# Ten modulation runs of the odd layer: from TensorE matmuls to ScalarE scaling and GpSimd adds

## The chip, the core and the metric

The kernel runs on one core of one Trainium2 chip. The metric is the device time of one execution in microseconds (us). Its engines are PE (TensorE: matrix products), DVE (VectorE), ACT (ScalarE), POOL (GpSimd) and SP (SyncE, which issues the loads). PEld is TensorE's load of weights, which runs beside its products.

## The reference, cut to what matters

Two blocks run one after the other on a stream x of 256 tokens by 1024. The first is a mixer with a mixture of experts; the change doesn't touch it. The second has two layers (0 even, 1 odd), each steered by a modulation that is computed from one vector c:

```python
cond = silu(c)                                       # 1 x 1024
for l in range(2):
    mod = cond @ ada_w[l] + ada_b[l]                 # 1024 -> 6144
    sh1, sc1, g1, sh2, sc2, g2 = split(mod, 6)
    h = rms_norm(x, norm_mix[l]) * (1 + sc1) + sh1
    y = even_mixer(h) if l % 2 == 0 else odd_mixer(h)    # attention
    x = x + g1 * (y @ w_out[l])
    h = rms_norm(x, norm_ffn[l]) * (1 + sc2) + sh2
    x = x + g2 * ((silu(h @ wg) * (h @ wu)) @ wd)    # feed-forward, 2816 wide
```

`ada_w` is 2 x 1024 x 6144 in fp32, 48 MB. The kernel reads it in 24 loads of 2 MB; load v gives half of one of the six vectors: layer v // 12, half v % 12. Loads 22 and 23 are the two halves of the odd layer's g2.

## The kernel before

**Loads.** All weights of the second block pass through five slots of 2 MB (`ring`). SP issues the loads in the order of `plan.loads`; load k takes the slot of load k - 5 and waits until that one is `freed`: for a product's weights until their last chunk is used, for a modulation weight until its run is done. SP issues in order, so a load that waits holds up all behind it.

**Chunks.** A product's weights are used in chunks of 1024 columns, numbered from 0 over the whole program. ACT copies chunk i to one of six buffers (`W_c_r`, `X_c_r`: the high part), DVE subtracts the copy from the weights (`ring_r`: the low part), PE multiplies three times (high, low, and the high weights with the low part of h). `begin(i)` on each of the three engines is chunk i's step, and behind it stands whatever the plan puts at the point ("f", i). On PE begin(i) comes five chunks ahead of the use. The even feed-forward has the gate and up chunks 62 to 105, four for each of 11 loads, and the down chunks 106 to 127; the odd layer follows with its key/value weights (kvo) 128 to 131, its two query halves 132 to 139, sixteen attention units, the output product 140 to 147 and its feed-forward from 148.

**Modulation.** `Plan.ada` (l. 143) puts a *run* at a point: PE multiplies the eight 128x512 slices of load v by silu(c), repeated over 32 columns (`csr`), into bank 7; ACT copies the bank to `acc`. `Plan.close` puts the *close* at a later point: PE sums `acc` over the partitions with four one-column products by `ones`, or, for loads 22 and 23, in row form with two products of 512 columns (`acc,ones` and `gates,ones`); then DVE adds the bias into `modc`, or ACT copies the row to `gates`. Bank 7 is shared, so each run waits until the close before it has been read. The even layer's g2 is in `modc`.

**Places.** Run 14 stands inside the normalisation at the head of the even feed-forward (`modulated`, between the sums and the broadcast), run 15 and the close of 14 at chunk 112, the close of 15 at 115, run 16 inside the normalisation of the odd layer, runs 17 to 23 at units 0, 2, ..., 12 of the odd attention, the closes at the units between.

**Stage boundaries.** When a product has ended, DVE forms 1 + scale times the gain (`prepare`, two small operations on `st`), adds the gated result to x in eight steps (`add_xT`, `x<-ps,modc,x`), ACT squares (`sc<-x`), PE sums over the partitions (`ones,sc`), DVE forms the inverse root (`st`, then `rb`, printed as `sc<-st`), PE broadcasts it (`ident,sc`), DVE and ACT normalise in eight steps (`R_c<-x,st,ps`, `hT_r<-R_c,modc`), and the next product starts.

**Names in the rows.** L1826 is PE's one matmul helper and L32 the helper of DVE, ACT and POOL, so tiles tell the operations apart. L651 and L678 are the load issues of gate/up and of the other weights.

## Time and profile before

| | |
|---|---|
| median of 3 runs | 1469.51 us (1468.12 to 1473.89) |
| the profiled execution | 1468.73 us, span 1467.0 us |
| mean granted clock of PE | 0.88 of full speed |
| PE busy | 1191.2 us (81%) |
| DVE busy | 615.8 us (42%) |
| ACT busy | 475.6 us (32%) |
| POOL busy | 7.6 us (1%), 54 instructions |
| chain that ended last | PE 57%, DMA 22%, DVE 12%, ACT 5% |

The span lies within the profiled execution's own time. Shares are averages over stages with different limits: the DMA share of the chain comes from the experts of the first block. The even feed-forward runs from about 925 to 1130, the odd attention from about 1172 to 1240. Granted clock 1.00 is TensorE's upper level (2.4 GHz), 0.50 the lower (1.2 GHz).

### The profile page before, as it was taken

The numbers are of one execution on the slowest core, as the hardware profiler recorded it, in microseconds if no ns is written. First come the engines' busy times: TensorE is split into PE (matmuls) and PEld (weight loads), VectorE is DVE, ScalarE is ACT, GpSimd is POOL, SyncE is SP. The second block draws the span as 40 slices with busy tenths as digits, with TensorE's granted clock in tenths as the row PEclk, the third lists the DMA queues.
The fourth block names the chain that finished last, engine by engine and source line by source line (L and its number), as shares of the span: only waits on it lengthen the run. The fifth ranks groups of instructions, "written<-read, shape, count | busy, mean of one in ns | idle before, by whom it ended". The sixth has DMA issues, their size and how long they took to land.

```text
span 1467.0 us, 19464 instructions
## 1 busy us (share of the span) xinstructions
PE 1191.2 (81%) x7703; PEld 874.9 (60%) x7703; DVE 615.8 (42%) x1240; ACT 475.6 (32%) x767; POOL 7.6 (1%) x54
## 2 busy tenths in 40 slices
PE   5888888575676756846897888999999978999998
PEld 4665565242332323413675438899898735999986
DVE  3473652010010000101663676655535656565553
ACT  4561621000000000002532335555433447455541
POOL 1000000000000000000000000000000000000000
PEclk9897888798888878978897678899999988999999
DMA  8542149999999999999446431865546472655520
GB/s 294 173 150 80 59 168 424 430 429 430 431 429 428 431 430 428 431 425 401 164 152 244 172 116 58 264 204 203 191 151 223 174 274 70 222 181 187 205 98 29
DMA packets 121729, 368.67 MB, mean 251 GB/s; under 512 B 9842, under 2 KB 56093, under 8 KB 110878
## 3 DMA queue, kind: packets, MB, share of 16 engines
q1 hardware_dynamic: 120556, 367.26, 65.1%
q8 instruction: 64, 1.05, 0.3%
q10 hardware_dynamic: 1074, 0.08, 0.1%
q14 instruction: 35, 0.29, 0.1%
HBM read 366.28 MB, written 1.05 MB: 250 GB/s over the span
## 4 chain that ended last, share of the span: by engine, by line
PE 57%; DMA 22%; DVE 12%; ACT 5%; issue 3%; SPq 1%; DVEq 0%; ACTq 0%
PE ps L1826 54%; DMA more<-in_w_gate_dram 8%; DMA more<-in_w_down_dram 7%; DMA more<-in_w_up_dram 6%; PE ps L1830 3%; DVE st L32 3%; DVE ring_r L32 2%; DVE R_c L32 2%; SPq L669 1%; DVE X_c L32 1%; DVE R_a L32 1%; DVE X_a L32 1%; ACT W_c_r L32 1%; ACT X_c L32 1%; DVE sc L32 1%
## 5 line engine op out<-in xcount | busy, mean ns | idle before, releaser
L1826 PE MATMUL ps<-hT_r,ring_r 128*128 128x256 f32 x864 | 243.7, 282 | 0.0
L1826 PE MATMUL ps<-ring,xg 128*32 128x512 f32 x640 | 140.1, 734 | 126.1 <-DMA more<-in_w_gate_dram 79.3
L1826 PEld LDWEIGHTS ps<-ring,xg 128*32 128x32 f32 x640 | 36.9, 132 | 222.3 <-issue 222.3
L1826 PEld LDWEIGHTS ps<-hT_r,ring_r 128*128 128x128 f32 x864 | 166.0, 192 | 0.0
L32 DVE TENSOR_TENSOR ring_r<-ring,W_c_r 128x1024 fp32r<-128x1024 f32 x94 | 115.2, 1225 | 96.3 <-ACT W_c_r L32 92.4
L1826 PE MATMUL ps<-R_c_r,W_c_r 128*128 128x256 f32 x608 | 152.7, 283 | 0.0
L32 DVE TENSOR_TENSOR ring_r<-ring,X_c_r 128x1024 fp32r<-128x1024 f32 x88 | 107.8, 1225 | 95.2 <-ACT X_c_r L32 92.3
L1826 PE MATMUL ps<-R_c_r,X_c_r 128*128 128x256 f32 x576 | 147.7, 284 | 0.0
L1826 PE MATMUL ps<-more,xg 128*32 128x512 f32 x384 | 134.6, 726 | 0.0
L32 ACT ACTIVATE W_c_r<-ring 128x1024 fp32r<-128x1024 f32 x94 | 99.7, 1060 | 87.3 <-PE ps L1826 83.0
L32 ACT ACTIVATE X_c_r<-ring 128x1024 fp32r<-128x1024 f32 x88 | 93.3, 1061 | 89.6 <-PE ps L1826 84.4
L32 DVE TENSOR_TENSOR x<-x,ps 128x512 f32<-128x512 f32 x36 | 24.8, 688 | 231.3 <-PE ps L1826 231.0
L1826 PE MATMUL ps<-hT_r,X_c_r 128*128 128x256 f32 x416 | 118.3, 284 | 2.9 <-DVE R_c_r L32 2.5
L1826 PE MATMUL ps<-hT_r,W_c_r 128*128 128x256 f32 x416 | 118.6, 285 | 1.9 <-DVE R_c_r L32 1.8
L1826 PEld LDWEIGHTS ps<-R_c_r,W_c_r 128*128 128x128 f32 x608 | 108.8, 190 | 0.0
L1826 PEld LDWEIGHTS ps<-R_c_r,X_c_r 128*128 128x128 f32 x576 | 104.0, 191 | 1.5 <-issue 1.5
L1826 PE MATMUL ps<-ring_r,hT_r 128*128 128x512 f32 (+1 forms) x240 | 94.8, 395 | 0.0
L1826 PEld LDWEIGHTS ps<-hT_r,X_c_r 128*128 128x128 f32 x416 | 78.8, 189 | 4.4 <-issue 3.0
L1826 PEld LDWEIGHTS ps<-hT_r,W_c_r 128*128 128x128 f32 x416 | 79.7, 191 | 2.7 <-DVE R_c_r L32 2.2
L1826 PE MATMUL ps<-ring,csr 128*32 128x512 f32 x384 | 63.6, 794 | 13.1 <-DVE modc L32 12.6
L1826 PE MATMUL ps<-ring,hid 128*32 128x512 f32 x320 | 60.2, 654 | 12.7 <-DMA more<-in_w_down_dram 11.6
L1826 PE MATMUL ps<-sel,hn 128*128 128x128 f32 x256 | 63.1, 410 | 2.1 <-DVE sel L32 2.1
(280 smaller groups left out, 1912.4 us busy)
## 6 DMA issues: line engine op xcount, KB each, us to landing
ring<-in_ada_w_dram SPq DMA_DIRECT2D x24, 2048.0 KB, 8.1
ring<-in_w_gate_dram SPq DMA_DIRECT2D x20, 2048.0 KB, 18.9
ring<-in_w_up_dram SPq DMA_DIRECT2D x20, 2048.0 KB, 20.0
ring<-in_w_down_dram SPq DMA_DIRECT2D x20, 2048.0 KB, 19.4
more<-in_w_gate_dram SPq DMA_DIRECT2D x12, 2048.0 KB, 27.9
more<-in_w_up_dram SPq DMA_DIRECT2D x12, 2048.0 KB, 28.4
more<-in_w_down_dram SPq DMA_DIRECT2D x12, 2048.0 KB, 27.9
ring<-in_ffn_gate_dram SPq DMA_DIRECT2D x22, 1024.0 KB, 5.9
```

The lines of the kernel that those rows point to most:

```text
L32: op(*args, **kw).then_inc(sem, 1)
L669: sp.dma_start(dst, src).then_inc(s_w[slot[k]], 16)
L1826: return pe.matmul(out, lhsT, rhs, start=start, stop=stop, skip_group_check=True)
L1830: return pe.transpose(out, in_, ident[0:n, 0:n])
```

## The change

Runs 14 to 23 become *pool runs* (`pool_run`). For one that is planned when the chunk list has length c: at the points ("f", c + 2) to ("f", c + 5) ACT multiplies two of the eight slices each, in place in the ring, by 32 silu(c) of their rows (`cs32`, one more small tile, `ring<-ring,cs` in the rows); POOL waits for the last of them and for the close of the run before, and adds the eight slices into `acc` with seven 128x512 additions, each waiting for the one before; at ("f", c + 11) PE closes as before, for load 23 at the first attention unit. The slot of such a load is freed by POOL's last addition. The c are 62, 70, ..., 126 in steps of 8, and 132; the closes stand at 73, 81, ..., 137.

The order of the loads changes with it: modulation load 14 stands ahead of the first gate/up load, 15 to 19 behind every second gate/up load, 20 to 22 behind the down loads 0, 2 and 4, 23 behind kvo. The output weights of the odd layer move from unit 8 to ahead of attention. Seven runs and their closes leave the attention.

```diff
@@ -145,6 +145,16 @@
         v = self.pending = len(self.ada_order)
         self.ada_order.append((v // 12, v % 12, self.load("ada", v // 12, v % 12)))
         self.rows.setdefault(point, []).append((v, "run"))
+    def pool_run(self):
+        v, c = len(self.ada_order), len(self.chunks)
+        self.ada_order.append((v // 12, v % 12, self.load("ada", v // 12, v % 12)))
+        self.pooled.append(v)
+        for z in range(4):
+            self.rows.setdefault(("f", c + 2 + z), []).append((v, z))
+        self.rows.setdefault(("u", 4, 0) if v == 23 else ("f", c + 11), []).append((v, "close"))
     def product(self, name, n, part=None):
         k = self.load("w", name)
@@ -170,23 +180,21 @@
             if u == wo_at:
                 self.out_loads(j)
-    def ffn(self, l, turn_run, run):
+    def ffn(self, l, gate_up_runs=(), down_runs=()):
         self.first["gu", l] = len(self.chunks)
         for u in range(11):
             k = self.load("gu", l, u)
             for q in (0, 2, 1, 3) if u == 0 else range(4):
                 self.feed(k, q)
-            if u == 0 and turn_run:
-                self.ada(("n", l, 3))
+            if u in gate_up_runs:
+                self.pool_run()
         self.first["dn", l] = len(self.chunks)
         for u in range(6):
             k = self.load("w", ("dn", l, u))
             for q in range(min(4, 22 - 4 * u)):
-                if run is not None and 4 * u + q == run:
-                    self.ada(("f", len(self.chunks)))
-                if run is not None and 4 * u + q == run + 3:
-                    self.close(("f", len(self.chunks)))
                 self.feed(k, q)
+            if u in down_runs:
+                self.pool_run()
@@ -218,18 +226,18 @@
     p.units(3, 8, (0, 2, 4, 6), 2, 1)
     p.close(("o", 1))
     p.out_proj(1)
-    p.ffn(0, True, 6)
+    p.pool_run()
+    p.ffn(0, (1, 3, 5, 7, 9), (0, 2, 4))
     k = p.load("w", "kvo")
     p.first["kvo"] = len(p.chunks)
     for q in range(4):
         p.feed(k, q)
-    p.ada(("n", 1, 0))
+    p.pool_run()
     p.product("q0", 4)
     p.product("q1", 4)
-    p.units(4, 16, (0, 2, 4, 6, 8, 10, 12), 8, 2)
-    p.close(("o", 2))
+    p.out_loads(2)
     p.out_proj(2)
-    p.ffn(1, False, None)
+    p.ffn(1)
     p.end = len(p.chunks)
     return p
@@ -397,7 +406,7 @@
         for i, (k, q) in enumerate(plan.chunks):
             freed[k] = (s_use, i + 1)
         for v, (_, _, k) in enumerate(plan.ada_order):
-            freed[k] = (s_ar, v + 1)
+            freed[k] = (s_acp if v in plan.pooled else s_ar, v + 1)
         for m, k in enumerate(plan.experts):
             freed[k] = (s_mm, m + 1)
@@ -788,6 +797,15 @@
             side.end()
+            for v in plan.pooled:
+                w = ring[:, slot[plan.ada_order[v][2]], :].rearrange("p (c n) -> p c n", c=8)
+                pool.wait_ge(s_ar, v + 1)
+                pool.wait_ge(s_ac, v)
+                G(pool.tensor_tensor, acc[:, :], w[:, 0, :], w[:, 1, :], ALU.add)
+                for c in range(2, 8):
+                    G(pool.tensor_tensor, acc[:, :], acc[:, :], w[:, c, :], ALU.add, up=s_acp if c == 7 else None)
         @block.scalar
         def scalar(act):
@@ -804,10 +822,19 @@
             def ada(point):
                 for v, what in plan.rows.get(point, ()):
                     l, i, k = plan.ada_order[v]
-                    if what == "run":
+                    if what in range(4):
+                        w = ring[:, slot[k], :].rearrange("p (c n) -> p c n", c=8)
+                        if what == 0:
+                            act.wait_ge(*landed[k])
+                            if v == plan.pooled[0]:
+                                act.wait_ge(s_cs, 1)
+                                copy(cs32[:, :], cs[:, :], scale=32.0)
+                        for c in (2 * what, 2 * what + 1):
+                            copy(w[:, c, :], w[:, c, :], scale=cs32[:, c:c + 1], up=s_ar if c == 7 else None)
+                    elif what == "run":
                         act.wait_ge(s_ar, v + 1)
                         copy(acc[:, :], ps[7][:, :], up=s_acp)
-                    elif row_gate(l, i):
+                    elif what == "close" and row_gate(l, i):
                         act.wait_ge(s_ac, v + 1)
                         copy(gates[:, 512 * (i % 2):512 * (i % 2) + 512], ps[7][:, :], up=s_gate)
@@ -1832,6 +1859,8 @@
             def ada(point):
                 for v, what in plan.rows.get(point, ()):
                     l, i, k = plan.ada_order[v]
+                    if what in range(4):
+                        continue
                     take(7)
                     if what == "run":
                         w = ring[:, slot[k], :].rearrange("p (c n) -> p c n", c=8)
```

Three places show what the planner makes of it. The first is ACT at the head of the even feed-forward, before; `hT_r<-ps,st` ends the normalisation of the even attention's output, `sc<-x` are the squares at the boundary:

```order
L32 ACTIVATE X_c_r<-ring 128x1024 x2
L32 ACTIVATE W_c_r<-ring 128x1024
L32 ACTIVATE X_c_r<-ring 128x1024
L32 ACTIVATE sc<-x 128x256 x8
L32 ACTIVATE hT_r<-R_c,modc 128x256 x8
L32 ACTIVATE acc<-ps 128x512
L32 ACTIVATE W_c_r<-ring 128x1024 x2
```

and after:

```order
L32 ACTIVATE X_c_r<-ring 128x1024 x2
L32 ACTIVATE W_c_r<-ring 128x1024
L32 ACTIVATE cs<-cs 128x8
L32 ACTIVATE ring<-ring,cs 128x512 x2
L32 ACTIVATE X_c_r<-ring 128x1024
L32 ACTIVATE ring<-ring,cs 128x512 x2
L32 ACTIVATE sc<-x 128x256 x8
L32 ACTIVATE hT_r<-R_c,modc 128x256 x8
L32 ACTIVATE W_c_r<-ring 128x1024
L32 ACTIVATE ring<-ring,cs 128x512 x2
```

Four scales of load 14 now stand among the chunk copies ahead of the squares, the other four between the next copies; the copy of bank 7 to `acc` is gone.

The second place is POOL's stream at its end, with the semaphores that each instruction waits for; `R_c` is a mask in the even attention. Before:

```order
L32 MEMSET qcol 64x1 [waits s_pool]
L32 MEMSET qcol 64x1 [waits s_slopes] x35
L32 MEMSET R_a 128x512 [waits s_slopes,s_k_decayed]
L32 AFFINE_SELECT R_c<-R_c 128x128 [waits s_slopes,s_index_sum]
L32 AFFINE_SELECT R_c<-R_c 128x256 [waits s_index_causal,s_index_sum]
```

and after, where `s_ada_run` is ACT's last scale of a run and `s_ada_closed` PE's close of the run before:

```order
L32 MEMSET R_a 128x512 [waits s_slopes,s_k_decayed]
L32 AFFINE_SELECT R_c<-R_c 128x128 [waits s_slopes,s_index_sum]
L32 AFFINE_SELECT R_c<-R_c 128x256 [waits s_index_causal,s_index_sum]
L32 TENSOR_TENSOR acc<-ring 128x512 [waits s_index_causal,s_ada_closed,s_ada_run]
L32 TENSOR_TENSOR acc<-acc,ring 128x512 [waits s_pool] x6
L32 TENSOR_TENSOR acc<-ring 128x512 [waits s_ada_copied,s_ada_closed,s_ada_run]
```

Ten groups of seven additions have come to the end of POOL's stream.

The third place is DVE at the end of the even feed-forward, where the last subtractions are those of the kvo chunks. Before:

```order
L32 TENSOR_TENSOR ring_r<-ring,W_c_r 128x1024 x2
L32 TENSOR_TENSOR ring_r<-ring,X_c_r 128x1024 x2
L32 TENSOR_TENSOR ring_r<-ring,W_c_r 128x1024
L32 TENSOR_TENSOR ring_r<-ring,X_c_r 128x1024
L32 TENSOR_SCALAR st<-modc 128x8
L32 TENSOR_TENSOR st<-st,cols 128x8
L32 SCALAR_TENSOR_TENSOR x<-ps,modc,x 128x256 x8
```

and after:

```order
L32 TENSOR_TENSOR ring_r<-ring,W_c_r 128x1024 x2
L32 TENSOR_TENSOR ring_r<-ring,X_c_r 128x1024 x2
L32 TENSOR_TENSOR modc<-ps,cols 128x4
L32 TENSOR_TENSOR ring_r<-ring,W_c_r 128x1024
L32 TENSOR_TENSOR ring_r<-ring,X_c_r 128x1024
L32 TENSOR_SCALAR st<-modc 128x8
L32 TENSOR_TENSOR st<-st,cols 128x8
L32 SCALAR_TENSOR_TENSOR x<-ps,modc,x 128x256 x8
```

The update of `modc` behind the close of run 21 now stands ahead of the last two subtractions and of the gated sum.

## Rows read from the trace of the kernel before

**Rows 1.** Windows: even feed-forward in two parts, odd attention, its end.

```profile
core 0: us, PE busy (x) PEld busy (x) DVE busy (x) ACT busy (x) POOL busy (x), PEclk, DMA share, GB/s
925.00:1055.00 130.00, 128.17 (x1064) 126.75 (x1060) 78.20 (x91) 67.72 (x85) 0.00 (x0) 0.98 0.64 212
1062.00:1132.00 70.00, 69.48 (x577) 65.89 (x577) 30.22 (x41) 24.09 (x28) 0.00 (x0) 0.98 0.54 189
1193.00:1224.00 31.00, 31.00 (x249) 16.06 (x246) 20.29 (x80) 21.91 (x62) 0.00 (x0) 1.00 0.77 272
1234.00:1237.00 3.00, 2.29 (x18) 1.26 (x16) 1.27 (x2) 2.25 (x5) 0.00 (x0) 0.52 0.02 5
```

**Rows 2.** Timeline of SP (start, duration): gate/up load 0, modulation load 14.

```profile
860.89 0.37 SPq L651 DMA_DIRECT2D ring<-in_ffn_gate_dram  x1
906.55 0.37 SPq L678 DMA_DIRECT2D ring<-in_ada_w_dram  x1
```

**Rows 3.** Load issues near 988 and 1010: KB, us to landing.

```profile
ring<-in_ffn_up_dram SPq DMA_DIRECT2D x1, 1024.0 KB, 8.0
...
ring<-in_ffn_down_dram SPq DMA_DIRECT2D x1, 2048.0 KB, 9.1
```

**Rows 4.** Timelines, head of the even feed-forward (start, us, idle before); a copy.

```profile
915.09 4.39 DVE L32 SCALAR_TENSOR_TENSOR x<-ps,modc,x 128x256 f32<-128x256 f32 x8
...
923.90 0.42 DVE L32 SCALAR_TENSOR_TENSOR sc<-st 128x256 f32<-128x256 f32 x1
...
922.22 3.64 PE L1826 MATMUL ps<-ring,csr 128*32 128x512 f32 x16
925.79 1.22 PE L1826 MATMUL ps<-ident,sc 128*128 128x128 f32 x4
928.78 0.36 PE L1826 MATMUL ps<-hT_r,X_c_r 128*128 128x256 f32 x1 [1.77 <-DVE R_c_r L32]
...
1047.57 0.63 ACT L32 ACTIVATE R_c_r<-sc 128x512 fp32r<-128x512 f32 x1 [1.43 <-DVE sc L32]
```

**Rows 5.** Timeline of PE at chunk 112: run 15.

```profile
1062.29 2.55 PE L1826 MATMUL ps<-ring,csr 128*32 128x512 f32 x16 [3.37 <-DVE modc L32]
```

**Rows 6.** Timeline of PE in the odd attention: a close, half a row close.

```profile
1204.99 1.05 PE L1826 MATMUL ps<-ones,acc 128*128 128x1 f32 x8
...
1216.60 1.12 PE L1826 MATMUL ps<-acc,ones 128*128 128x512 f32 x2
```

**Rows 7.** Timelines of DVE and PE at the boundary to the odd layer.

```profile
1123.63 4.39 DVE L32 SCALAR_TENSOR_TENSOR x<-ps,modc,x 128x256 f32<-128x256 f32 x8
...
1126.27 3.63 PE L1826 MATMUL ps<-ones,sc 128*128 128x1 f32 x32
...
1134.46 0.47 PE L1826 MATMUL ps<-X_c_r,hT_r 128*128 128x512 f32 x1 [1.77 <-DVE R_c_r L32]
```

**Rows 8.** Odd attention: DVE at units 3 and 15, a run, ACT's last pair.

```profile
1195.42 0.17 DVE L32 COPY X_c<-st 128x2 f32<-128x2 f32 x1
1230.03 0.17 DVE L32 COPY X_c<-st 128x2 f32<-128x2 f32 x1
...
1201.77 1.92 PE L1826 MATMUL ps<-ring,csr 128*32 128x512 f32 x16
...
1227.40 0.51 ACT L32 ACTIVATE X_c<-X_c,s 128x257 f32<-128x257 f32 x1
1231.65 0.51 ACT L32 ACTIVATE X_c<-X_c,s 128x257 f32<-128x257 f32 x1
```

**Rows 9.** Groups by line and shape: POOL's selects, DVE's subtraction, ACT's copy.

```profile
L32 POOL TENSOR_SCALAR_AFFINE_SELECT negd<-negd 128x256 f32<-128x256 f32 x1 | 0.4, 401 | 0.5 <-DVE negd L32 0.5
L32 POOL TENSOR_SCALAR_AFFINE_SELECT ident<-ident 128x128 f32<-128x128 f32 x1 | 0.3, 293 | 0.2 <-POOL ident L32 0.2
...
L32 DVE TENSOR_TENSOR ring_r<-ring,W_c_r 128x1024 fp32r<-128x1024 f32 x94 | 115.2, 1225 | 96.3 <-ACT W_c_r L32 92.4
...
L32 ACT ACTIVATE W_c_r<-ring 128x1024 fp32r<-128x1024 f32 x94 | 99.7, 1060 | 87.3 <-PE ps L1826 83.0
```

More of the change, by code:

```diff
@@ L125, in __init__ @@
     def __init__(self):
-        self.loads, self.ada_order, self.rows = [], [], {}
+        self.loads, self.ada_order, self.rows, self.pooled = [], [], {}, []
         self.chunks, self.first = [], {}
@@ L282, in build @@
         cs = sb("cs", [128, 8])
+        cs32 = sb("cs32", [128, 8])
         acc = sb("acc", [128, 512])
```

## The prediction

> **What bounds the kernel now.** I read the windows first, stage by stage, then the timelines at the stage boundaries, then the loads. In the even feed-forward PE is busy 128.2 of 130 us at a granted clock of 0.98, and 69.5 of 70 us in its second part [rows 1]: PE sets the pace, and whatever is added to its stream there is paid in full. A chunk of 1024 weight columns, 24 products, is used every 2.83 us (69.5 us less a close, for 577 products, gives 2.85, some cold ones among them); VectorE is busy 78 of the 130 us, ScalarE 68, GpSimd not at all. In the odd attention PE is again full, 31.0 of 31 us at clock 1.00 [rows 1], while the modulation runs are in it; behind the last run it falls to 0.52 [rows 1]. Between the stages stands a chain: the last chunks split on ScalarE and VectorE, VectorE adds the gated result to x, ScalarE squares, PE sums, VectorE normalises, PE starts [rows 4, 7]. So the change is worth what it does to PE in the two full stretches, to these chains, and to the loads, since the slot of a modulation weight now comes free only when GpSimd has done its adds.
>
> **The price of an add.** The whole case hangs on it. Call p the time of one of the 70 adds (128x512, each waiting for the one before). No row shows GpSimd adding two operands. Its one-operand rows are 401 ns at 256 elements and 293 ns at 128 [rows 9], so 0.185 us plus 0.84 ns an element: 0.62 us for one operand of 512, 1.05 if the second operand doubles the per-element part, 1.2 with a hand-over of 0.15 between dependent instructions. So p alone lies between 0.75 and 1.2; I take 1.2, since the adds have two operands. Beside it VectorE runs a subtraction of two SBUF operands, 1.23 us [rows 9], in every 2.83 us. If the two engines cannot read at once, an add gets 1.60 of every 2.83 us and costs 1.2 x 2.83 / 1.60 = 2.1; if each add waits out a whole subtraction, 2.43; where PE stalls and VectorE idles, 1.2. Between 1.2 and 2.43 no row decides. I take 1.9, near the middle, because the loop below contains idle stretches of VectorE. The Trainium skill, SBUF — State Buffer, section "Who interferes with whom", speaks against this change: it says a VectorE instruction with two SBUF inputs contends with a GpSimd instruction that reads SBUF, and the loser waits for the whole instruction. By it p would be 1.9 or more; no run here shows it yet. The Trainium skill, GPSIMD Engine Reference, section 3.1, gives 4497 ns for an add of 2048 fp32 elements, by which I estimate 1.1 us for 512 with nothing beside it; no row here shows that either.
>
> **The change part by part.** The sum is made against the profiled run, 1468.73 us, 0.8 below the median of 1469.51.
>
> *Start of the even feed-forward.* The first gate/up load was issued at 860.89 [rows 2]. Now a modulation load stands ahead of it on SyncE and takes that slot; the gate/up load gets the slot freed at 906.55 [rows 2] and lands some 8.5 us later (0.4 to issue the first half, 8.0 for the second [rows 2, 3]), near 915.2. Its four chunk copies stand on ScalarE, and their subtractions on VectorE, ahead of the gated sum that started at 915.09 [rows 4]. Four copies at 1.17 (1.06 and the gap [rows 9]), the scaled condition and four weight scales (priced by the 0.63 us of a 128x512 copy [rows 4], 0.72 with its gap) end near 923, so the gated sum starts near 923.4: +8.3. PE's run, 3.64 us at the slower clock, held the broadcast until 925.79 though VectorE had its input at 924.32 [rows 4]: without it -1.4. **+6.9** (6.4 to 7.4).
>
> *The stall at chunk 112* goes: PE waited 3.37 us for VectorE and ran 2.55 us [rows 5], with a few cold matmuls behind it. **-6.3** (-5.9 to -6.6).
>
> *Closes.* Seven stand in the full stretch instead of two, at 1.05 us [rows 6]: **+5.2**. The row form of the tenth-but-one costs two pairs of 1.12 us [rows 6] beside the query product: **+2.2**. The last one falls into PE's idle time before attention: nothing, or 2.2 without that cover.
>
> *Boundary to the odd layer.* PE's last features end at 1126.3 [rows 7]; VectorE had both last subtractions done before and started the gated sum at 1123.63. Now the update behind the close of the eighth run stands on VectorE ahead of the last two subtractions, and PE makes that close only a chunk or so before the end; two subtractions, the two small operations and the sum follow: start 4.5 us behind PE's end, not 2.7 before it, +7.2; and PE, idle longer, makes its 3.63 us of sums [rows 7] cold, +1.4. **+8.6** (7.2 to 13). The run that stood here was hidden.
>
> *Odd attention.* Six pairs of units took 34.6 us, 5.77 each [rows 8]. A run of 1.92 and a close of 1.05 [rows 6, 8] leave PE 2.8 of it. Then ScalarE binds, 4.25 a pair as in the last two [rows 8]; or PE falls to half clock and needs about 5.4. Middle: -5.8 over six pairs (-2 to -9.1). Before them the stall of the first runs, where VectorE's third unit began at 1195.42 [rows 8], loses 7.2. **-13** (-9 to -16.5).
>
> *Loads and adds.* This is the new wait. Slot of one modulation weight freed, the gate/up load into it lands 8.6 us later (8.4 [rows 2, 3] and a wake-up of SyncE), ScalarE copies two chunks of it and makes the last four scales of the next modulation weight (2 x 1.17 + 4 x 0.70 = 5.15), GpSimd adds for 7p, the next slot is free. The loop takes 13.75 + 7p per eight chunks; PE needs 8 x 2.83 + 1.05 = 23.7. It breaks even at **p = 1.41**. The first run's scales end 11.7 us into the stage (behind ScalarE's eight normalising steps, two copies and four scales), so its adds end at 11.7 + 7p; PE reaches its close at 19.1.
> With p = 1.9 the first adds end at 25.0, the loop takes 27.05, the eighth ends at 25.0 + 7 x 27.05 + 1.8 (three down loads at 9.1 instead of 8.4 [rows 3]) = 216.2. Only then may the key/value load start: landed at 225.4, four copies and six scales 8.9, the last subtraction 1.4, two small operations 0.3, then 10.8 from the gated sum to PE's start as before [rows 7], 1.1 for cold sums: PE starts the odd layer at 247.9, where it was 1134.46 - 928.78 = 205.7 [rows 4, 7]. **+42**, which swallows the closes, the stall at chunk 112 and the boundary. Cover for nothing: GpSimd has no other work there.
>
> **Sum of the forecast:** +6.9 + 42.2 + 2.2 - 13 = +38, **1507 us**.
>
> **The rivals.**
> *PE-bound, not slower.* The adds run beside VectorE undisturbed, p = 1.25. The loop, 22.5, hides under PE's 23.7; one stall of 7 x 1.25 - 7.4 = 1.4 at the first close. Sum: 6.9 + 1.4 + 5.2 - 6.3 + 8.6 + 2.2 - 13 = +5.0: **1474** (1468 to 1479), within 0.5%. It decides below p = 1.41. For it: VectorE is idle 52 of the stage's 130 us [rows 1], and a one-operand op of GpSimd is short [rows 9]. Against it: only 0.2 us an add of spare.
> *Part of the way.* p = 1.6: the first adds end at 22.9, the loop takes 24.95, the eighth ends at 199.4, PE starts 31.7 later at 231.1, +25.4. Sum +21.5: **1490**.
> *Faster.* Adds undisturbed at p below 1.2, ScalarE binding in attention at 4.25 (-16.5), the boundary covered by PE's later end (0 instead of +8.6): 6.9 + 5.2 - 6.6 + 2.2 - 16.5 = -8.8, **1460**. Against it: VectorE's order puts the update ahead of the last two subtractions.
> *Attention gives nothing back.* PE at half clock holds 5.4 a pair, the clock having fallen as soon as the runs ended [rows 1]: 4 us more in each case, inside the ranges.
>
> **Chances.** Turn-taking 0.52 (1495 to 1525; p = 2.2 gives a loop of 29.15 and 1524), part of the way 0.16, PE-bound 0.25, faster 0.07. The range, 1467 to 1525, leaves out the faster case and p above 2.2. This kernel's measurement tells 0.5%, 7.3 us, from no change; the PE-bound case lies within it but for its upper edge. So faster 0.07, same 0.22, slower 0.71.
>
> **What the profile after would show.** GpSimd's adds: mean well over 1.4 us and longer beside VectorE's subtractions than alone, or all alike near 1.2. VectorE's subtractions: some over 1.23. In the windows of the even feed-forward PE under 0.9 with waits released by ScalarE or VectorE behind late loads, and gate/up loads issued more than 23.7 us apart in pairs; or PE full, and only the boundary longer. The gated sum starting near 923. Attention pairs between 4.25 and 5.4. I am wrong if GpSimd's two-operand add costs under 1.4 beside VectorE, or if loads are not what waits.

## The result, and the profile after

The changed kernel takes 1522.12 us (median of four, 1518.72 to 1527.81) against 1469.59 us: a ratio of 1.036 (95% interval 1.033 to 1.038), 53 us slower. The profiled execution took 1519.07 us with a span of 1517.0. One execution further on, of the first VectorE version, fell into a slow state (2129.3 us) and is left out of its median.

The span falls into six stretches, each between two rows that every kernel here has: SyncE's issue into the slot that the even output weights free (906.55 in before, [rows 2]), the feed-forward's first product and the odd layer's ([rows 4, 7]), VectorE's first copy in the first and in the last attention unit ([rows 8] for the last), the end. PE's helper, L1826 in the kernel before, stands at L1853 here and at other lines in the experiments.

| us | ahead | head | even feed-forward and boundary | query products | attention units | tail | span |
|---|---|---|---|---|---|---|---|
| before | 906.55 | 22.23 | 205.68 | 44.46 | 51.11 | 236.97 | 1467.0 |
| after | 909.20 | 29.43 | 245.65 | 56.55 | 39.03 | 237.14 | 1517.0 |
| difference | +2.65 | +7.20 | +39.97 | +12.09 | -12.08 | +0.17 | +50.0 |

The attention gives back what was hoped for it, and the query products ahead of it take just that away; the feed-forward loses 40 us.

The windows of after (columns as in [rows 1]) show the feed-forward in two parts, the query products and the attention:

```profile
core 0: us, PE busy (x) PEld busy (x) DVE busy (x) ACT busy (x) POOL busy (x), PEclk, DMA share, GB/s
938.00:1058.00 120.00, 109.67 (x856) 109.18 (x857) 77.53 (x75) 77.01 (x101) 49.25 (x29) 0.91 0.61 203
1058.00:1163.00 105.00, 96.97 (x794) 96.36 (x792) 54.34 (x43) 54.85 (x66) 48.95 (x28) 0.96 0.61 226
...
1185.00:1225.00 40.00, 32.80 (x124) 25.29 (x123) 29.49 (x47) 21.79 (x30) 9.88 (x7) 0.87 0.52 184
...
1252.00:1290.00 38.00, 29.32 (x188) 17.41 (x187) 28.16 (x98) 26.88 (x76) 0.00 (x0) 0.72 0.00 1
```

PE was full in [rows 1]; now it is busy 91 to 92% of the feed-forward, and its granted clock is 0.91 and 0.96 instead of 0.98. In the attention, where it was full, it is busy 77% at 0.72. GpSimd's timeline (start, us, idle before) shows what sets the pace, the first and the eighth pool run, and the ninth:

```profile
950.54 1.30 POOL L32 TENSOR_TENSOR acc<-ring 128x512 f32<-128x512 f32 x1 [105.69 <-ACT ring L32]
951.92 11.50 POOL L32 TENSOR_TENSOR acc<-acc,ring 128x512 f32<-128x512 f32 x6
...
1137.22 1.30 POOL L32 TENSOR_TENSOR acc<-ring 128x512 f32<-128x512 f32 x1 [13.44 <-ACT ring L32]
1138.60 11.61 POOL L32 TENSOR_TENSOR acc<-acc,ring 128x512 f32<-128x512 f32 x6
1170.24 1.27 POOL L32 TENSOR_TENSOR acc<-ring 128x512 f32<-128x512 f32 x1 [20.03 <-ACT ring L32]
1171.59 7.99 POOL L32 TENSOR_TENSOR acc<-acc,ring 128x512 f32<-128x512 f32 x6
```

The eight runs of the feed-forward start (1137.22 - 950.54) / 7 = 26.67 us apart, where PE's eight chunks and a close need 23.7 by the forecast, and 23.5 in the run with one add below. Each holds its slot 12.4 us or more with its adds: 12.4 in the second to sixth run, 12.9, 14.0 and 13.0 in the first, seventh and eighth (1138.60 + 11.61 - 1137.22 = 12.99), 12.7 on average. SyncE's timeline shows what hangs on that: gate/up load 3 is issued 0.03 us behind the first run's last add (951.92 + 11.50 = 963.42), and the key/value load 0.03 us behind the eighth's (1150.21).

```profile
963.45 0.37 SPq L660 DMA_DIRECT2D ring<-in_ffn_gate_dram  x1
...
1150.24 0.37 SPq L687 DMA_DIRECT2D ring<-in_w_in_odd_dram  x1
```

The view of waits, PE in the feed-forward (us in total, times, longest), names the adds too, for which the closes wait. In the kernel before the same view named VectorE's `modc`, 3.4 us, the stall of [rows 5], which is gone:

```profile
PE ps L1853 <- POOL acc L32: 14.5, 6, 5.7
```

And the adds and VectorE's subtractions hold each other up. The timelines of both in the third run, and VectorE's beside the ninth:

```profile
1003.33 1.29 POOL L32 TENSOR_TENSOR acc<-ring 128x512 f32<-128x512 f32 x1 [13.69 <-ACT ring L32]
...
1007.44 2.15 POOL L32 TENSOR_TENSOR acc<-acc,ring 128x512 f32<-128x512 f32 x1
...
1003.56 0.95 DVE L32 TENSOR_TENSOR sc<-sc,ps 128x256 f32<-128x256 f32 x2 [0.56 <-ACT sc L32]
1006.38 2.07 DVE L32 TENSOR_TENSOR ring_r<-ring,W_c_r 128x1024 fp32r<-128x1024 f32 x1 [1.87 <-ACT W_c_r L32]
1008.55 1.59 DVE L32 TENSOR_TENSOR R_c_r<-sc,R_c_r 128x512 fp32r<-128x512 f32 x1
...
1170.42 4.40 DVE L32 SCALAR_TENSOR_TENSOR x<-ps,modc,x 128x256 f32<-128x256 f32 x8
```

Beside nothing, or beside a VectorE operation with one operand in PSUM (`sc<-sc,ps`, `x<-ps,modc,x`, whose 4.40 us are the 4.39 of [rows 7]), an add takes 1.27 to 1.30 us and the next begins 1.34 to 1.38 behind it, 1.35 on average in the ninth run, whose seven take 9.34 (1171.59 + 7.99 - 1170.24). Where adds and subtractions with both operands in SBUF take turns, the add takes 2.15 us and the subtraction 2.07 to 2.14 instead of 1.23 [rows 9]; the product of two SBUF operands behind it takes 1.59 instead of 0.69.

At the boundary the timelines of DVE and PE answer to [rows 7]:

```profile
1168.69 1.23 DVE L32 TENSOR_TENSOR ring_r<-ring,X_c_r 128x1024 fp32r<-128x1024 f32 x1 [1.45 <-ACT X_c_r L32]
...
1158.82 0.95 PE L1853 MATMUL ps<-ones,acc 128*128 128x1 f32 x8
1171.50 6.96 PE L1853 MATMUL ps<-ones,sc 128*128 128x1 f32 x32 [11.74 <-ACT sc L32]
...
1184.28 0.77 PE L1853 MATMUL ps<-X_c_r,hT_r 128*128 128x512 f32 x1 [1.77 <-DVE R_c_r L32]
```

PE ends the even feed-forward at 1159.8 and starts the odd layer 24.5 us later; before it was 8.2. It waits 11.74 us, for key/value weights that came late, and then makes its sums at the lower level of the clock (0.50 is granted there), 6.96 us instead of 3.63. So of the 40.0 us 16.3 lie at the boundary and 11.1 in PE's waits ahead of it (14.5 instead of 3.4). In the rest, some 12 us, PE is busy longer, with five closes more, one run less and the lower granted clock; no run tells these apart.

### The profile page after: what moved, and what is told of

Same layout as the page of the kernel before. It is cut to its first block and busy times, and to the rows that moved or that the text cites. A ratio compares the mean times of both kernels' runs of the same rounds, so it can differ in the third digit from the quotient of the medians.

```text
span 1517.0 us, 19285 instructions
## 1 busy us (share of the span) xinstructions
PE 1192.5 (79%) x7543; PEld 891.4 (59%) x7543; DVE 652.6 (43%) x1240; ACT 526.6 (35%) x838; POOL 124.5 (8%) x124
## 5 line engine op out<-in xcount | busy, mean ns | idle before, releaser
L1853 PE MATMUL ps<-hT_r,ring_r 128*128 128x256 f32 x864 | 249.7, 289 | 0.0
L1853 PE MATMUL ps<-ring,xg 128*32 128x512 f32 x640 | 140.2, 736 | 131.1 <-DMA more<-in_w_gate_dram 83.8
L1853 PEld LDWEIGHTS ps<-ring,xg 128*32 128x32 f32 x640 | 36.7, 132 | 227.5 <-issue 227.5
L32 DVE TENSOR_TENSOR ring_r<-ring,X_c_r 128x1024 fp32r<-128x1024 f32 x88 | 119.8, 1361 | 116.9 <-ACT X_c_r L32 113.8
L32 DVE TENSOR_TENSOR ring_r<-ring,W_c_r 128x1024 fp32r<-128x1024 f32 x94 | 129.5, 1378 | 90.0 <-ACT W_c_r L32 85.7
L1853 PEld LDWEIGHTS ps<-hT_r,ring_r 128*128 128x128 f32 x864 | 168.1, 195 | 0.0
L1853 PE MATMUL ps<-R_c_r,W_c_r 128*128 128x256 f32 x608 | 154.4, 286 | 0.0
L1853 PE MATMUL ps<-R_c_r,X_c_r 128*128 128x256 f32 x576 | 147.0, 283 | 0.0
L1853 PE MATMUL ps<-more,xg 128*32 128x512 f32 x384 | 134.8, 723 | 0.0
L32 DVE TENSOR_TENSOR x<-x,ps 128x512 f32<-128x512 f32 x36 | 24.8, 688 | 234.0 <-PE ps L1853 233.7
L1853 PE MATMUL ps<-hT_r,X_c_r 128*128 128x256 f32 x416 | 121.0, 291 | 1.8 <-DVE R_c_r L32 1.8
L1853 PE MATMUL ps<-hT_r,W_c_r 128*128 128x256 f32 x416 | 120.1, 289 | 2.4 <-DVE R_c_r L32 2.3
L1853 PEld LDWEIGHTS ps<-R_c_r,W_c_r 128*128 128x128 f32 x608 | 113.2, 198 | 0.0
L1853 PEld LDWEIGHTS ps<-R_c_r,X_c_r 128*128 128x128 f32 x576 | 106.8, 195 | 0.0
L32 POOL TENSOR_TENSOR acc<-acc,ring 128x512 f32<-128x512 f32 x60 | 104.0, 1734 | 4.7
L1853 PE MATMUL ps<-ring_r,hT_r 128*128 128x512 f32 (+1 forms) x240 | 95.7, 399 | 0.0
L1853 PEld LDWEIGHTS ps<-hT_r,X_c_r 128*128 128x128 f32 x416 | 82.0, 197 | 2.6 <-issue 2.5
L1853 PEld LDWEIGHTS ps<-hT_r,W_c_r 128*128 128x128 f32 x416 | 80.8, 194 | 3.0 <-DVE R_c_r L32 2.5
L1853 PE MATMUL ps<-ring,hid 128*32 128x512 f32 x320 | 58.1, 650 | 14.6 <-DMA more<-in_w_down_dram 13.7
L1853 PE MATMUL ps<-sel,hn 128*128 128x128 f32 x256 | 62.8, 410 | 2.1 <-DVE sel L32 2.1
```

The costliest lines, as they stand in the source:

```text
L32: op(*args, **kw).then_inc(sem, 1)
L1853: return pe.matmul(out, lhsT, rhs, start=start, stop=stop, skip_group_check=True)
```

## The experiments

All compare with the kernel before, run beside them. For the stage lengths the rows of the table above are read in each profile, which is of one execution and not always of the median one (1513.98 us for 20 memsets, 1515.02 for the last run with one add, 1505.92 for the gate/up load first, 1480.31 for 64 bytes more).

| us | ahead | head | feed-forward | query | units | tail | median |
|---|---|---|---|---|---|---|---|
| one add a run | 916.19 | 29.66 | 213.60 | 48.47 | 38.63 | 237.45 | 1486.06 |
| 14 memsets a run | 910.17 | 29.67 | 215.33 | 51.98 | 39.05 | 237.50 | 1485.98 |
| 20 memsets a run | 916.99 | 29.62 | 237.17 | 51.99 | 39.01 | 237.12 | 1507.85 |
| last run one add | 912.07 | 29.60 | 246.42 | 48.53 | 39.14 | 237.24 | 1517.95 |
| gate/up load first | 909.06 | 20.81 | 241.36 | 56.30 | 38.65 | 237.72 | 1508.26 |
| before, again | 906.92 | 22.21 | 206.03 | 44.41 | 51.03 | 237.00 | 1469.42 |
| before, 32 bytes more | 914.50 | 22.24 | 208.43 | 43.46 | 52.45 | 237.02 | 1479.75 |
| before, 64 bytes more | 916.09 | 21.64 | 207.07 | 44.84 | 50.91 | 238.05 | 1474.63 |
| after without new tile | 905.61 | 29.64 | 244.75 | 56.92 | 39.14 | 237.24 | 1516.23 |
| VectorE sums, first | 915.87 | 20.18 | 227.99 | 49.43 | 38.84 | 236.09 | 1490.14 |
| VectorE sums, second | 908.13 | 20.97 | 222.12 | 46.36 | 38.44 | 236.88 | 1474.22 |
| mixed | 912.12 | 22.23 | 204.99 | 43.50 | 40.89 | 237.57 | 1461.72 |

**The adds against the rest of the change.** One add a run:

```diff
-                G(pool.tensor_tensor, acc[:, :], w[:, 0, :], w[:, 1, :], ALU.add)
-                for c in range(2, 8):
-                    G(pool.tensor_tensor, acc[:, :], acc[:, :], w[:, c, :], ALU.add, up=s_acp if c == 7 else None)
+                G(pool.tensor_tensor, acc[:, :], w[:, 0, :], w[:, 1, :], ALU.add, up=s_acp)
```

> Leaves out six of GpSimd's seven additions of each pool run, so the odd layer's modulation is wrong; everything else of the change stays (80 weight scales on ScalarE, closes, order of the loads). My theory, the loop of slot, load, two copies with four scales, seven adds: the adds shrink from 12.4 to 1.4 us, the loop from 26.7 to about 15.6, under PE's 23.7. Then only the small terms are left (head of the even feed-forward +7.8, closes +5.2, the stall at chunk 112 gone -6.3, boundary about +8.6, query products up to +5, odd attention -12): 1470 to 1480 us, the pool runs 23.7 apart, PE over 0.97 busy in the even feed-forward. Rival, the scales, closes and moved loads cost the time and not the adds: 1495 us or more.

Measured: 1486.06 us, 1.010 times before (1.006 to 1.014). The feed-forward falls from 245.65 to 213.60: the loop is what cost there. PE is full:

```profile
969.80:1009.80 40.00, 40.00 (x342) 40.00 (x341) 23.79 (x28) 29.76 (x39) 2.59 (x2) 1.00 0.88 291
```

The remaining +7.9 fit the prediction's closes, stall and boundary (5.2 - 6.3 + 8.6 = 7.5), which without the adds stand in the open. The timelines of VectorE and PE at the boundary show the update of `modc` waiting for PE ahead of the last subtractions, as forecast:

```profile
1142.06 0.16 DVE L32 TENSOR_TENSOR modc<-ps,cols 128x4 f32<-128x4 f32 x1 [9.73 <-PE ps L1851]
1142.32 2.18 DVE L32 TENSOR_TENSOR ring_r<-ring,W_c_r 128x1024 fp32r<-128x1024 f32 x1
1144.61 1.23 DVE L32 TENSOR_TENSOR ring_r<-ring,X_c_r 128x1024 fp32r<-128x1024 f32 x1
...
1146.34 4.39 DVE L32 SCALAR_TENSOR_TENSOR x<-ps,modc,x 128x256 f32<-128x256 f32 x8
...
1141.07 0.95 PE L1851 MATMUL ps<-ones,acc 128*128 128x1 f32 x8
1147.42 6.96 PE L1851 MATMUL ps<-ones,sc 128*128 128x1 f32 x32 [5.40 <-ACT sc L32]
...
1159.45 0.77 PE L1851 MATMUL ps<-X_c_r,hT_r 128*128 128x512 f32 x1 [1.77 <-DVE R_c_r L32]
```

The gated sum starts 4.3 us behind PE's end at 1142.02 (4.5 forecast), and PE needs 17.4 us from there to the odd layer instead of 8.2. The pool runs in the middle of the feed-forward start 23.5 us apart, which is PE's own pace. GpSimd's timeline:

```profile
1045.24 1.29 POOL L32 TENSOR_TENSOR acc<-ring 128x512 f32<-128x512 f32 x1 [22.23 <-ACT ring L32]
...
1068.76 1.29 POOL L32 TENSOR_TENSOR acc<-ring 128x512 f32<-128x512 f32 x1 [22.23 <-ACT ring L32]
```

The stages after "ahead" sum to 7.4 us more than before, as expected; that the time is 6 us over the range lies in the 9.6 us ahead of them, which the expectation did not have.

**Time of the slot or reads of GpSimd?** The seven adds became 14 memsets of the same tile, then 20:

```diff
...
+                for c in range(14):
+                    G(pool.memset, acc[:, :], 0.0, up=s_acp if c == 13 else None)
```

> In place of each run's seven additions GpSimd writes 14 memsets of 128x512 into the same tile, which read nothing (the sums are left out, the odd layer's modulation is wrong). By the memset row of before, 0.54 us and a gap, 14 take about 8.7 us, near the 9.45 that seven adds take with nothing beside them. My theory, GpSimd's reads and VectorE's second SBUF operand shut each other out: VectorE's subtractions stay at 1.23 us beside the memsets, the loop is 14.2 + 8.7 = 22.9, PE sets the pace: 1472 to 1482 us. Rival, any work of GpSimd slows VectorE: subtractions near 2.1 us beside the memsets, loop over 25, 1500 us or more.

> As the run with 14 memsets, but with 20 of them, about 12.4 us: the slot is held as long as by the seven additions in the changed kernel, and GpSimd still reads nothing (sums left out). My theory, the time that the slot is held is what costs: loop about 26, the odd layer starts some 38 to 50 us later than before, 1503 to 1522 us, although no subtraction is over 1.3 us. Rival, VectorE's own lengthened subtractions are what holds PE up: with them gone the time falls under 1485 us.

Measured: 1485.98 and 1507.85 us. The 14 memsets take 8.13 us a run, the feed-forward 215.33; the 20 take 11.63, and the feed-forward is back at 237.17 with every subtraction at 1.23 us there. The groups by line and shape (the last columns: busy, mean ns, idle before) of the run with 20 memsets, and of after:

```profile
L32 DVE TENSOR_TENSOR ring_r<-ring,W_c_r 128x1024 fp32r<-128x1024 f32 x94 | 115.2, 1225 | 106.3 <-ACT W_c_r L32 102.6 <-DVE x L32 0.5
```

```profile
L32 DVE TENSOR_TENSOR ring_r<-ring,W_c_r 128x1024 fp32r<-128x1024 f32 x94 | 129.5, 1378 | 90.0 <-ACT W_c_r L32 85.7 <-DVE x L32 0.5
```

So it is the time for which the slot is held that costs, and VectorE's own lengthening costs little by itself: 31.5 of the 40.0 us come without any, and the other 8.5 are about what the adds hold the slot longer, 8 x (12.7 - 11.6). What the reads do is to make seven adds 12.4 us long or more instead of 9.34. The median of the 14 memsets is 4 us over the expected range, by 3.6 us ahead and 7.5 us in the query products; there the memsets, which only write, lengthened VectorE's scalar operation and its copies, and nothing with two operands:

```profile
1178.06 1.09 DVE L32 TENSOR_SCALAR st<-st 128x8 f32<-128x8 f32 x2
1179.18 0.37 DVE L32 TENSOR_TENSOR st<-st 128x8 f32<-128x8 f32 x2
...
1182.64 2.53 DVE L32 COPY R_c<-R_c 128x256 f32<-128x256 f32 x4
```

**The query products.** The last run's adds reduced to one:

```diff
...
+                if v == 23:
+                    G(pool.tensor_tensor, acc[:, :], w[:, 0, :], w[:, 1, :], ALU.add, up=s_acp)
+                    continue
```

> The changed kernel, but load 23 gets one addition instead of seven (half of the odd layer's g2 is wrong). In the changed kernel its adds stand beside VectorE's small operations of the query head norm, of which two-operand ones take 0.67 us instead of 0.17, and attention's first unit starts 56.6 us behind the layer's first product instead of 44.5. My theory, GpSimd's adds hold up these small operations: they are short again, the first unit starts 6 to 10 us earlier, 1510 to 1515 us. Rival, the query weights' late load and the cold clock stretch this stage: the first unit moves by under 2 us, 1519 us or more.

Measured: 1517.95 us (1.032, 1.027 to 1.037). The first unit moves from 56.55 to 48.53, 8.0 us earlier, inside the expectation. The time falls by only 4 and is 3 us over the expected range: this kernel too lost more ahead (912.07), and its profile (1515.02) lies below its median. VectorE's timeline in after, and in this run, over the same operations of the head norm:

```profile
1207.16 1.50 DVE L32 TENSOR_SCALAR st<-st 128x8 f32<-128x8 f32 x2
1208.70 1.35 DVE L32 TENSOR_TENSOR st<-st 128x8 f32<-128x8 f32 x2
1210.09 1.54 DVE L32 SCALAR_TENSOR_TENSOR st<-st 128x8 f32<-128x8 f32 x3
1211.66 1.12 DVE L32 TENSOR_TENSOR st<-st 128x8 f32<-128x8 f32 x1
```

```profile
1210.98 0.38 DVE L32 TENSOR_SCALAR st<-st 128x8 f32<-128x8 f32 x2
1211.39 0.37 DVE L32 TENSOR_TENSOR st<-st 128x8 f32<-128x8 f32 x2
1211.79 0.57 DVE L32 SCALAR_TENSOR_TENSOR st<-st 128x8 f32<-128x8 f32 x3
1212.40 0.17 DVE L32 TENSOR_TENSOR st<-st 128x8 f32<-128x8 f32 x1
```

An operation of eight elements a partition takes 0.17 us alone. Taken one by one in the trace of after, one that starts as an add ends takes 0.17 there too, and the one behind it, which meets the next add, takes 1.12 to 1.30, nearly the whole of that add (the 1.35 of the second line are 0.17 and 1.15). So the 0.67 of the expectation is a mean of the two. Four of the nine operations of this chain paid it, with one operand or two, and the products behind it began 4.9 us later. The rest of the 8.0 us lies behind the chain, where the next product of two SBUF operands took 1.63 us instead of 0.69, and the granted clock of these 40 us was 0.87 instead of 0.96.

**The head.** Gate/up load 0 ahead of modulation load 14 again, that load's scales two chunks later:

```diff
+            if u == 0 and early:
+                self.pool_run(2)
...
-    p.pool_run()
-    p.ffn(0, (1, 3, 5, 7, 9), (0, 2, 4))
+    p.ffn(0, (1, 3, 5, 7, 9), (0, 2, 4), True)
```

> The changed kernel, but gate/up load 0 stands ahead of modulation load 14 again, and load 14's scales stand two chunks later (points 66 to 69, close at 75). My theory: the head of the even feed-forward (from the freed slot of the even output weights to the first product) takes 21 to 22 us as in before or 1 less, not 29.4; the first adds start some 6 us earlier and, since the loop sets the pace, the odd layer too: 1513 to 1517 us. Rival, the head is set by something else (the scales on ScalarE): it stays near 29 us and the time at 1519 to 1523.

Measured: 1508.26 us (1.027, 1.024 to 1.030), the head 20.81 instead of 29.43, the feed-forward 241.36: 8.6 and 4.3 us less. That is the forecast's direction and more than its size: the median lies 5 us below the expected range. The order of two loads, with the scales two chunks later, was worth 14 us in the median.

**What is lost ahead of the change.** The slot of the even output weights came free at 909.20 in after and at 910 to 917 in the first four experiments, although nothing of the change stands ahead of it. Four kernels test that: before, unchanged; before with an unused tile of the size of `cs32`, and of twice that size,

```diff
+        cs32 = sb("cs32", [128, 8])
         acc = sb("acc", [128, 512])
```

and the changed kernel with `cs32` in the router's weights, which are free by then:

```diff
-        cs32 = sb("cs32", [128, 8])
+        cs32 = wr[:, 0, 0:8]
```

> The kernel before, unchanged, profiled once more. Five profiles of changed kernels reach the issue at 906.55 of before (the slot of the even output weights) 2.7 to 10.4 us later, though nothing ahead of it was changed. If this is the scatter of single executions, a second profile of before also moves by several us there, and its stages after it repeat: 205.7 us from the feed-forward's first product to the odd layer's, 44.5 to the first attention unit, 51.1 to the last, each within 1 us. If the changed kernels lose it by themselves, this profile repeats 906.5 within 1 us.

> The kernel before with one more tile, 32 bytes in each partition (cs32 of the change), that nothing uses; it moves every tile behind it by 32 bytes, the second part of the expert weights' buffer among them. Theory: this shift is what the changed kernels lose ahead of any instruction that the change moves (2.5 to 10 us by their profiles, while two profiles of before agree within 0.4): the slot of the even output weights comes free at 909 to 917 instead of 906.6 and the time is 1472 to 1480 us. Rival, it is something else (code, GpSimd's longer program): 906.5 to 907, 1469 us as before.

> The kernel before with an unused tile of 64 bytes in each partition instead of 32. If what cost 10 us in the median with the 32-byte tile is where the tiles behind it begin modulo 64 bytes, 64 bytes bring them back: slot of the even output weights free at 906 to 907, 1468 to 1471 us. If any shift of the addresses costs it, or a full partition, 909 or more and 1474 to 1481 us as with 32.

> The changed kernel with its scaled condition in 32 bytes of the router's weights, free by then, in place of the new tile; so all tiles lie where they lay before. Theory of the shift: the slot of the even output weights comes free at 906 to 907 as in before, and the time falls by 3 to 8 us, to 1514 to 1519. Rival: 909 or more, 1520 to 1523 us as the change.

Measured: 906.92 and 1469.42 us; 914.50 and 1479.75; 916.09 and 1474.63; 905.61 and 1516.23. An unused tile of 32 bytes makes the kernel before slower (1.004, 1.003 to 1.006; its times stand in two groups, about 1474 and 1480), one of 64 bytes too (1.003, 1.001 to 1.005; its groups are the same). Without its tile the change takes 6 us less in the median, but four executions each, 1515 to 1520 and 1519 to 1528, don't keep the two apart. The profile of the 64-byte kernel (1480.31) is of its upper group, both of before are near that kernel's median, and single executions of before also took up to 1480: so scatter has a part in the differences of single profiles, though it doesn't explain the medians. That 64 bytes don't bring back the old time speaks against a start modulo 64 bytes; a larger unit, with a tile of 256 bytes for example, was not tried.

The views of waits show where the time goes: PE waits for the weights of the experts in the first block (`more`, one of the tiles that the new one moves). In the first 905 us, before and with 32 bytes more (us in total, times, longest):

```profile
PE ps L1826 <- DMA more<-in_w_gate_dram: 79.3, 7, 12.5
PE ps L1826 <- DMA more<-in_w_up_dram: 46.0, 7, 8.2
PE ps L1826 <- DMA more<-in_w_down_dram: 14.1, 6, 6.8
...
PE ps L1827 <- DMA more<-in_w_gate_dram: 85.4, 7, 12.5
PE ps L1827 <- DMA more<-in_w_up_dram: 48.6, 8, 7.5
PE ps L1827 <- DMA more<-in_w_down_dram: 17.5, 9, 8.2
```

The three sum to 139.4 us before, 151.5 with 32 bytes more, 141.1 in the changed kernel without its tile, and 150.0 in the last version below, which has no new tile either. That the tile has a part in it is shown; through what it acts is not, and it is not the whole: two later kernels without the tile reached the slot at 908.13 and 912.12. This stays open.

**VectorE in place of GpSimd.** VectorE multiplies and adds in one instruction, so ScalarE's scales go as well:

```diff
+                    if what in range(4):
...
+                            V(ts, own, w[:, 0, :], cs32[:, 0:1], None, ALU.mult)
+                        for c in (2 * what, 2 * what + 1):
+                            if c:
+                                V(stt, out=own, in0=w[:, c, :], scalar=cs32[:, c:c + 1], in1=own, op0=ALU.mult, op1=ALU.add,
+                                  up=s_acp if c == 7 else None)
...
-        self.rows.setdefault(("u", 4, 0) if v == 23 else ("f", c + 11), []).append((v, "close"))
+        self.rows.setdefault(("u", 4, 0) if v == 23 else ("f", c + 7), []).append((v, "close"))
```

> GpSimd and ScalarE are out: VectorE makes each pool run itself, eight multiply-adds of 128x512 (weights times silu(c), added to the accumulator), two behind each of four chunk subtractions, and frees the slot; gate/up load 0 stands ahead of load 14; PE closes seven points behind the run's place instead of eleven, so that run 21's update leaves the boundary; run 22 moves ahead of the last down load but one. Each multiply-add should take about 0.69 us as VectorE's other 128x512 operations of two SBUF operands do; 1.38 and 1.23 fit into a chunk's 2.83. Theory (the cost of the change was the slot's loop and GpSimd's reads beside VectorE): head 21 to 22 us, 206 to 209 from there to the odd layer, 45 to 49 to the first unit, 39 for the units: 1455 to 1466 us, faster than before. Rival, VectorE becomes the bound in the even feed-forward: over 215 us there, 1470 or more.

Measured: 1490.14 us (1.013, 1.009 to 1.017). The head is 20.18, but the feed-forward 227.99, far from the expectation. Two places stand out. PE waited for VectorE at the first close, and ScalarE, ahead of the last chunk copy, for PE's row close; the timelines of PE and ACT:

```profile
955.42 1.84 PE L1851 MATMUL ps<-ones,acc 128*128 128x1 f32 x8 [5.88 <-DVE acc L32]
...
1147.39 0.60 ACT L32 ACTIVATE gates<-ps 128x512 f32<-128x512 f32 x1 [9.28 <-PE ps L1851]
```

The second version moves run 14 two points later, run 15 one, the row close of load 22 to 133, and has no new tile:

```diff
-                self.pool_run(2)
+                self.pool_run(4)
...
-        self.rows.setdefault(("u", 4, 0) if v == 23 else ("f", c + 7), []).append((v, "close"))
+        self.rows.setdefault(("u", 4, 0) if v == 23 else ("f", 133 if v == 22 else c + 7), []).append((v, "close"))
```

> The version in which VectorE makes the runs, with three places mended: load 14's multiply-adds stand at points 68 to 71 (the first close made PE wait 5.9 us for VectorE), load 15's one chunk later, and the row close of load 22 stands at 133, behind the boundary (at 130 ScalarE waited 9.3 us for it ahead of the last chunk copy). The scaled condition takes 32 bytes of the router's weights in place of a new tile. Expected if those waits were all: head 20 to 21 us, 206 to 210 to the odd layer, 45 to 49 to the first unit, 39 for the units, and nothing lost ahead of the change: 1455 to 1464 us, faster than before. Rival, VectorE's runs cost PE's stream more than that (closes waited for at every run): over 214 us in the feed-forward, 1465 or more.

Measured: 1474.22 us (1.003, 1.001 to 1.005), another miss: the feed-forward takes 222.12. Seven closes still waited for VectorE, 0.4 to 2.5 us each and 8.6 in all, and the row close, moved behind the boundary, takes 3.8 us at the lower clock ahead of the odd layer's first product. The rival named in the expectation holds. It led to the last version: only loads 15 to 20 go to VectorE, with closes nine points behind; 14 and 21 stay PE runs inside the two normalisations, 22 and 23 at attention units 4 and 8.

```diff
+            if u == 0 and early:
+                self.ada(("n", l, 3))
+            if u == 1 and early:
+                self.close(("f", len(self.chunks) + 1))
...
+    p.ffn(0, (1, 3, 5, 7, 9), (0,), True)
...
+    p.ada(("n", 1, 0))
...
+    p.units(4, 16, (4, 8), 6, 2)
```

> A version from what the runs so far showed: only loads 15 to 20 are made by VectorE in the even feed-forward (two multiply-adds behind each of four subtractions, close nine points behind the run's place, so that PE doesn't wait for it); 14 and 21 stay PE runs inside the two normalisations, where before hid them; 22 and 23 stay PE runs at attention units 4 and 8, where PE is idle a quarter of the time without runs; no new tile. Theory: head 22 us as before, 205 to 208 to the odd layer (five closes more, the stall at chunk 112 gone), 44.5 to the first unit, 40 to 43 for the units, nothing lost ahead: 1457 to 1463 us, faster than before by 0.5 to 0.8%. Rival, VectorE's multiply-adds hold up PE's stream all the same, or each run in attention costs 3 us or more: 1466 or more.

Measured: 1461.72 us, 0.993 times before (0.991 to 0.996), 8 us faster, as expected. Its groups by line show a multiply-add's price, 752 ns; the subtractions stay at 1.23 us, and the closes in the feed-forward wait for nothing:

```profile
L32 DVE SCALAR_TENSOR_TENSOR acc<-ring,wr,acc 128x512 f32<-128x512 f32 x42 | 31.6, 752 | 1.5
```

The gain is the attention's: 40.89 instead of 51.11 with two runs in it instead of seven, and 204.99 instead of 205.68 in the feed-forward. Its profile loses 5.6 us ahead, against the expectation.

## Why the prediction was right, and where it was not

The forecast, turn-taking of adds and subtractions that makes the slot loop the bound, was right: 1507 us forecast, 1522 measured, inside the range. The runs with one add and with memsets show that the time for which the adds hold the slot sets the loop. That the time came near the upper edge of the range is not the doing of the adds, which cost less than forecast. By its own steps:

- *Price of an add.* Taken at 1.9, measured 12.7 / 7 = 1.82 in the feed-forward, 1.77 in most runs. The value with nothing beside it, 1.2, was too low: 1.35, an operation of 1.27 and a hand-over of 0.08, for which the forecast had put 0.15, a figure that no row of before shows. An alternating add and subtraction take 2.23 us together (2.15 and a gap), less than the sum of both alone, 1.35 + 1.23 = 2.58. The Trainium skill's rule (SBUF — State Buffer, "Who interferes with whom") is borne out here: two SBUF operands of VectorE against GpSimd's reads lengthen both (2.07 to 2.14 and 2.15 us), one operand in PSUM does not (4.40 us), and memsets leave subtractions at 1.23. If the loser waited for the whole instruction, as the prediction has it, a pair would take 2.58 by these rows; the trace has 2.23. The prediction's estimate of 1.1 us from the Trainium skill, GPSIMD Engine Reference, section 3.1, was low beside the 1.27 to 1.30 of the trace.
- *Loop.* Forecast 27.05 a run, measured 26.67, of which 14.0 are not adds (13.75 forecast). PE's own pace was 23.5, not 23.7. With both, the loop breaks even at (23.5 - 14.0) / 7 = 1.36 us an add, not 1.41: the adds alone, at 1.35, would have stood just at the edge. The memsets of 8.13 us lie below it and let PE set the pace. PE's waits were for the adds themselves, at the closes, where the forecast had named ScalarE or VectorE behind late loads; and PE stood at 0.91 to 0.92, not under 0.9.
- *Feed-forward with boundary.* +42.2 forecast, +40.0 measured. The first adds ended 24.8 us into the stage (25.0 forecast), the eighth 211.6 (216.2), and PE started the odd layer 34.1 behind that (31.7), the cold sums costing 3.3 instead of 1.1. An earlier end and a longer boundary cancel in part here; that the two forecasts agree so well is luck.
- *Head.* +6.9 forecast, +7.2 measured: the gated sum started 16.3 us behind the freed slot instead of 8.5, +7.8 (8.3 forecast), and the way from there to the first product took 0.6 less (1.4 forecast). With the load first again the first part goes, and the head is 1.4 shorter than before.
- *Stall at chunk 112, closes, boundary.* Swallowed by the loop, as said; 7.5 forecast for the three, 7.9 measured with one add a run, the boundary in it at +9.2 (8.6 forecast).
- *Attention.* -13 forecast, -12.1 measured. Six pairs of units took 29.4 us, 4.90 each, between the two bounds of 4.25 and 5.4: -5.2 (-5.8 forecast). The stall of the first runs gave back 6.9 (7.2).
- *Query products.* This is the mis-sized term: +2.2 forecast, **+12.1 measured**. The step named the row close and left out that GpSimd's adds of the last run stand beside a chain of small VectorE operations. They cost 8.0, as the run with one add there shows; the other 4.1 remain with one add: the row close, scales and a cold start, not told apart.
- *Ahead.* Nothing forecast, +2.65 in the profile, and about 3 more in the median than in the profiled execution (1522.12 against 1519.07). A tile of 32 bytes can have a part in it; why is open.

The sum: 38.3 forecast, 50.0 in the profile; 9.9 of the difference are the query products, 2.65 lie ahead, the rest cancels. The rival in which PE stays the bound needed adds under 1.36 us beside VectorE; it falls. That of half the clock in attention, 4 us more, did not come: the term missed by 0.9, at a granted clock of 0.72.

## What to carry to other kernels

Work that is moved to an idle engine costs what it holds: here not GpSimd's time, but a load slot for 12.7 us of a loop that had none to spare; write the loop of slot, load, use and release down before the move, and its break-even. An idle engine is not a free one when it reads the memory that a busier one reads with two operands; look for chains of tiny operations beside it, where one can wait for a whole foreign instruction. And where several places can hide the same work, use each up to its slack: the version that won left four of ten runs where PE was idle or waiting anyway.

## What the runs showed of the hardware that was not expected

- GpSimd adds of 128x512 lengthen VectorE operations of eight elements that meet them from 0.17 to between 1.12 and 1.30 us, about as much as large ones (0.9); memsets, which read nothing, lengthen scalar operations (1.09 for two instead of 0.38) and copies (2.53 for four instead of 1.28), and leave those of two operands as they are (0.37 for two small ones, 1.23 for a subtraction).
- An unused tile of 32 or 64 bytes a partition, allocated in the middle, made the kernel before 10 and 4 us slower in the median. In the profiles 8.0 and 9.5 of the 11 to 12 us lie ahead of the stages that the change touches, where PE waits longer for the experts' weights (151.5 us with 32 bytes instead of 139.4).
